# Attention heads of a two-layer encoder trunk: half a weight block of matmuls between the transposes of the two query halves

## The reference

```
for l in range(2):
    h = rms_norm(x, norm_mix_g[l])
    proj = h @ w_in[l]                      # lru_x, lru_g, dq, dk, dv, sq, sk, sv
    o_lru  = rglru_branch(...)
    # 8 differential heads, 64 wide in q and k, 128 wide in v
    p = softmax(mask(q @ k.T * scale + bias)); attn = p[0] - lam * p[1]; o_diff = attn @ v
    # 16 sliding-window heads in 2 groups, 64 wide, with a sink logit
    p = softmax(concat([q @ k.T * scale + bias, sink]))[..., :-1];      o_swa  = p @ v
    gates = sigmoid(h @ w_gate[l] + b_gate[l])
    x = x + sum(gates * (branches @ w_branch[l])) @ w_out[l]
    x = x + peer_ffn(rms_norm(x, norm_ffn_g[l]))
```

## Time and profile before

| | |
|---|---|
| median of 3 runs | 2584.67 us (2582.19 to 2586.20) |
| profiled execution, its own time | 2584.68 us |
| its span (first to last instruction) | 2582.5 us |
| PE busy, PEld busy | 94%, 87% of the span |
| DVE, ACT busy | 68%, 60% of the span |
| head stage of layer 0, T0 of head 0 to T0 of head 15 | 199.46 to 308.60 us |
| the same of layer 1 | 1485.19 to 1594.30 us |

### The profile page before, as it was taken

The page is one execution under the profiler, slowest core; times in us unless marked ns, Lnnn a source line. Parts: engine busy times, 40 slices in busy tenths (PEclk is TensorE's granted clock), DMA queues, the critical chain, the costliest instruction groups (busy, mean ns, idle before and its releaser), DMA issues.

```text
span 2582.5 us, 53628 instructions
## 1 busy us (share of the span) xinstructions
PE 2428.9 (94%) x16770; PEld 2237.4 (87%) x16770; DVE 1764.3 (68%) x4132; ACT 1558.0 (60%) x3530; POOL 31.1 (1%) x96
## 2 busy tenths in 40 slices
PE   8998999999999679999999999999999986899998
PEld 8997889999999568888899988899999985688887
DVE  5666764877765986666656667648777659766666
ACT  5567745655555865555555677455555558655555
POOL 0000100000000000000000001000000000000000
PEclk9999999999999999999999999999999999999999
DMA  6554444455554015555544443545555440255554
GB/s 216 190 180 131 133 161 169 163 183 185 184 172 153 0 68 193 194 195 195 194 153 168 168 147 121 174 147 180 186 187 179 167 142 0 96 190 190 191 194 170
DMA packets 116446, 413.66 MB, mean 160 GB/s; under 512 B 8028, under 2 KB 18196, under 8 KB 116116
## 3 DMA queue, kind: packets, MB, share of 16 engines
q1 hardware_dynamic: 115860, 412.44, 46.6%
q10 hardware_dynamic: 512, 0.29, 0.0%
HBM read 411.09 MB, written 4.23 MB: 161 GB/s over the span
## 4 chain that ended last, share of the span: by engine, by line
PE 83%; DVE 9%; ACT 4%; issue 3%; DVEq 1%; DMA 0%; ACTq 0%; POOL 0%; POOLq 0%
PE bank L282 16%; PE bank L284 16%; PE bank L283 16%; PE bank L297 10%; PE bank L298 9%; PE bank L299 9%; DVE hot L1427 3%; DVE w_lo L264 1%; DVE hot L1431 1%; ACT w_hi L251 1%; DVE A L1437 1%; PE bank L374 1%; ACT L324 1%; PE bank L1047 1%; DVEq L1431 1%
## 5 line engine op out<-in xcount | busy, mean ns | idle before, releaser
L264 DVE TENSOR_TENSOR w_lo<-raw,w_hi 128x512 fp32r<-128x512 f32 x1512 | 1028.1, 689 | 744.8 <-ACT w_hi L251 731.8
L251 ACT ACTIVATE w_hi<-raw 128x512 fp32r<-128x512 f32 x1512 | 905.3, 626 | 376.0 <-PE bank L299 310.6
L282 PE MATMUL bank<-h_hi,w_hi 128*128 128x256 f32 x3360 | 963.5, 287 | 14.1 <-DVE w_lo L264 14.0
L283 PE MATMUL bank<-h_lo,w_hi 128*128 128x256 f32 x3360 | 953.8, 284 | 0.0
L284 PE MATMUL bank<-h_hi,w_lo 128*128 128x256 f32 x3360 | 953.7, 284 | 0.0
L282 PEld LDWEIGHTS bank<-h_hi,w_hi 128*128 128x128 f32 x3360 | 647.2, 193 | 23.4 <-DVE w_lo L264 16.6
L283 PEld LDWEIGHTS bank<-h_lo,w_hi 128*128 128x128 f32 x3360 | 647.7, 193 | 0.5
L284 PEld LDWEIGHTS bank<-h_hi,w_lo 128*128 128x128 f32 x3360 | 647.5, 193 | 0.0
L297 PE MATMUL bank<-w_hi,a_hi 128*128 128x512 f32 x1088 | 425.4, 391 | 8.3 <-issue 5.0
L298 PE MATMUL bank<-w_lo,a_hi 128*128 128x512 f32 x1088 | 424.8, 390 | 0.0
L299 PE MATMUL bank<-w_hi,a_lo 128*128 128x512 f32 x1088 | 424.5, 390 | 0.0
(11 more groups left out here) (186 smaller groups left out, 1980.6 us busy)
## 6 DMA issues: line engine op xcount, KB each, us to landing
raw<-stream SPq DMA_DIRECT2D x378, 1024.0 KB, 4.9
hank<-rel_hankel SPq DMA_DIRECT2D x16, 256.0 KB, 2.7
rel_hankel<-rel_line SPq DMA_DIRECT2D x16, 192.0 KB
hank<-rel_hankel SPq DMA_DIRECT2D x16, 128.0 KB, 2.1
A<-subkeys SPq DMA_DIRECT2D x2, 1024.0 KB, 5.0
x<-x_in SPq DMA_DIRECT2D x2, 512.0 KB, 4.2
pr<-lru_w SPq DMA_DIRECT2D x2, 512.0 KB, 8.2
out<-x SPq DMA_DIRECT2D x4, 256.0 KB, 2.0
```

The source lines that it names most:

```text
L251: act.activation(w_hi[:, (ring % 2) * 2 + k, :], raw[:, slot, sub, 512 * k:512 * k + 512], ACT.Copy).then_inc(w_hi_done, 1)
L264: dve.tensor_tensor(w_lo[:, q, :], raw[:, slot, sub, 512 * k:512 * k + 512], w_hi[:, q, :].bitcast(F32), ALU.subtract).then_inc(w_parts, 1)
L282: pe.matmul(ps, hi, rhs_hi(4 * k + c), start=first, stop=False)
L283: pe.matmul(ps, hi, rhs_lo(4 * k + c), start=False, stop=False)
```

## The change

On PE, `transpose_p` takes the query half t as an argument. T0 is followed by half H, then comes T1, then half H+1. On ACT the read-out `read_turned` takes t as well: T0 is read, then `w_hi` of H' is made, then T1 is read. Nothing else moves, no instruction is added or removed, and DVE, POOL and SP are unchanged.

```diff
@@ ACT @@
-                def read_turned(m):
+                def read_turned(m, t):
...
-                    for t in range(TT):
-                        act.wait_ge(pt_done.sem, pt_done.base + 2 * m + t + 1)
...
+                    act.wait_ge(pt_done.sem, pt_done.base + 2 * m + t + 1)
...
-                    read_turned(m)
+                    read_turned(m, 0)
                     H = HALVES[m + 1]
                     split_to(H, H + 1)
+                    read_turned(m, 1)
                     if m < 15:
                         exps(m + 1, 0)
@@ PE @@
-                def transpose_p(m):
+                def transpose_p(m, t):
...
                     H = HALVES[m]
-                    transpose_p(m)
-                    halves(H, H + 2)
+                    transpose_p(m, 0)
+                    halves(H, H + 1)
+                    transpose_p(m, 1)
+                    halves(H + 1, H + 2)
                     values(m)
```

More of the change, by code:

```diff
@@ L672, in exps @@
                     ins.then_inc(exp_done.sem, 1)
-                def read_turned(m):
+                def read_turned(m, t):
                     swa = m >= HEADS_DIFF
-                    for t in range(TT):
-                        act.wait_ge(pt_done.sem, pt_done.base + 2 * m + t + 1)
-                        T = bank[6 + t][:, :].rearrange("p (a b) -> p a b", a=4)
-                        pick = (slice(0, 4) if t else slice(0, 4, 2)) if swa else slice(0, t + 1)
-                        act.activation(prob_t[:, t, pick, :], T[:, pick, :], ACT.Copy).then_inc(pt_read.sem, 1)
+                    act.wait_ge(pt_done.sem, pt_done.base + 2 * m + t + 1)
+                    T = bank[6 + t][:, :].rearrange("p (a b) -> p a b", a=4)
+                    pick = (slice(0, 4) if t else slice(0, 4, 2)) if swa else slice(0, t + 1)
+                    act.activation(prob_t[:, t, pick, :], T[:, pick, :], ACT.Copy).then_inc(pt_read.sem, 1)
                 def read_values(m):
@@ L1035, in scores @@
                             pe.matmul(bank[2 + 2 * s + c][:, P * t + lo:P * t + hi], q[r, P * t:P * t + P], k[r, lo:hi], start=True, stop=True).then_inc(scored.sem, 1)
-                def transpose_p(m):
+                def transpose_p(m, t):
                     s, swa = m % 2, m >= HEADS_DIFF
[L1040 to L1048, removed]
+                    pe.wait_ge(attn_done.sem, attn_done.base + 2 * m + t + 1)
+                    if m:
+                        pe.wait_ge(pv_read.sem, pv_read.base + 2 * (m - 1) + t + 1)
+                    for c in range(2 if swa else 1):
+                        for kt in range(t + 1):
+                            at = P * (2 * c + kt)
+                            ins = pe.transpose(bank[6 + t][:, at:at + P], prob(s, t)[:, c, P * kt:P * kt + P], ident)
+                    ins.then_inc(pt_done.sem, 1)
                 def values(m):
```

## The result

| | before | changed |
|---|---|---|
| median | 2584.1 us (2581.1 to 2586.4) | 2590.1 us (2587.5 to 2591.9) |
| ratio to before, 95% interval | | 1.0023 (1.0016 to 1.0030) |
| span of the profiled execution | 2582.5 us | 2586.6 us |

The kernel became slower by 6.0 us, 0.23%. Run again beside other kernels, the ratio was 1.0012 (1.0003 to 1.0021), so the size is known less well than the first interval says; the sign is not in doubt. The page hardly shows it: the busy shares are those of before.

A forecast was written before the change was run, and what follows sets the result against it. One loop through T1, ACT's list and `weigh_probs` sets each head's period, PE's branch being about equally long. Losses of 4.9 us in layer 0 and 4.4 in layer 1 make 9.3 us: 2594.0 us, range 2587.5 to 2600.

The forecast's parts named there:

- the second rival: Whole kernel: nothing measurable, since gate waits in heads 13 and 15 and low-clock stretches shrink; 2588.7 us; chance 0.10.
- One of the signs that the prediction named for being wrong: Differential heads, head stages: the prediction is wrong if their period stays at 7.25 us or falls.
- T0 to T1: Head stages: T0 to T1 becomes 1.60 us in differential heads (0.84 before), 1.70 in sliding-window heads (0.66 before).
- The upper end of 0.1 us a head: Half behind a single transpose: switch costs 0.20 us instead of 0.10, adding 2.8 us in both layers.
- PE's gain turns into a wait at T0: Differential heads: PE's shorter branch (3.30 us for 4.01) becomes idle time of about 0.6 us before T0.
- Differential heads: Heads 1 to 7: T1 0.76 us later less 0.52 of `w_hi`, 0.24 us a head, 1.7 us a layer.
- Sliding-window heads: Heads 8 to 12: period 7.41 us, losing 0.16 or 0.25 us each, together 1.1 us a layer.
- Head 13: T1 queued behind half H, which waits for DVE's gate product: 8.92 us against 7.87, 1.05 us lost.
- the third rival: More than forecast: one or two more lower-clock stretches at 1.49 us each and a dearer switch; 2599.8 us; chance 0.10.
- Heads 14 and 15: T0 of head 14 to values of head 15: gate product wait delays T1, 10.74 us against 9.89, 0.85 lost.
- Heads 0 and 1 of layer 1: Head 0 loses 0.7 us, about as much returns in head 1's lower-clock stretch; counted as 0.
- The decision point named there: Softer form of the first rival: T1 less than 0.52 us later, meaning a half in under 1.26 us, not 1.50.

The follow-up runs named there:

- PE's part alone: PE in the new order (T0, half H, T1, half H+1), ACT in its order of before, against the changed kernel; 2604.5 us, ratio to before 1.0075.
- kernel with these heads alone: The kernel before, with the new order of both engines in heads 13 and 15 only; 2587.4 us, ratio to before 1.0012.
- kernel with three groups: T1 after three of the four groups of half H, against the kernel with T1 in the middle of half H; 2575.3 us, ratio to before 0.9964.

## Why the prediction was right, and where its sum was off

The direction and the range held: 2590.1 us lies in 2587.5 to 2600, and slower by over 0.2% came true, though only just; in the second measurement it was 0.12%. That T1 heads ACT's list and ACT's list sets the next head is borne out by the runs that move T1. But the head stages grew by 5.0 us where the sum said 9.3, and without the stretch at the lower clock in head 13 of layer 1 by some 3.8. The measured time lies nearer to the second rival (2588.7 us) than to the forecast (2594.0), and that the clock took a further 1.2 us there, which the sum did not hold, was luck for the number.

One of the signs that the prediction named for being wrong came: the period of differential heads fell, from 7.25 to 7.20 us. In these heads the change costs nothing, and all of the loss lies in the sliding-window heads, most of it in heads 13 to 15.

- *T0 to T1.* Forecast 1.60 and 1.70 us, measured 1.61 and 1.71. A half behind a single transpose starts without any further price. The upper end of 0.1 us a head was not needed.
- *PE's gain turns into a wait at T0.* Forecast about 0.6 us idle there, measured 0.63. The kernel with PE's part alone shows it to the hundredth: 7.72 us.
- *Differential heads: the term that failed.* Forecast +0.24 us a head, measured -0.05. The working took over 0.71 us for the two read-outs of the values up to `w_hi` (226.62 to 227.33). In this 0.71 ACT waits about 0.2 for PE's second product, t=1. With PE ahead the pair takes 0.50. The source view of the two read-outs, before and in the changed kernel (ns of one: least, median, most; first and last start), shows them 0.45 us apart before and 0.25 after:

```profile
L691 ACT ACTIVATE o_own<-bank,small x2: 367/367/367, 226.6 to 227.1; 128x128 f32<-128x128 f32 x2
L690 ACT ACTIVATE o_own<-bank,small x2: 347/350/352, 227.4 to 227.7; 128x128 f32<-128x128 f32 x2
```

(The hundredths come from the earlier trace rows and the timeline after: the pair ends 0.81 us behind its start before, 0.60 after, and the last of it lasts 0.37 and 0.35.) For sliding-window heads the prediction saw the same wait, since there a row names it (0.20), and took it out; in differential heads the two read-outs stand in one merged row, x2 with 0.81 us, and it was missed. A second, smaller part: ACT starts the read-out 0.42 us behind T1 now, 0.48 before. Together that is 0.27 us, of the 0.29 by which a head was misjudged, in 13 heads 3.8 us.
- *Sliding-window heads.* Forecast 7.41 us, measured 7.33: 0.05 us from the same distance between T1 and its read-out (0.64 us for 0.69), 0.03 from the two read-outs of the values. Their loss was 0.6 us a layer, not 1.1.
- *Head 13.* Forecast 8.92 us, measured 8.78 in layer 0, and half H 1.68 us behind T0 for 1.71. The kernel with these heads alone gives 8.90 and 8.83. In layer 1 the changed kernel lost 1.2 us more to a stretch at the lower clock; such a stretch was part of the third rival, which put one or two at 1.5 us each.
- *Heads 14 and 15.* Forecast 0.85 us, measured 0.85 and 0.77.
- *Heads 0 and 1 of layer 1.* Forecast 0, measured -0.26: the stretch at the lower clock stayed in head 1, and PE's shorter branch hid half of it (8.03 us for 8.74).

Of the rivals, the first (PE's order sets the period, 2566 us) fell in its strong form. But its time was almost reached by the kernel with T1 in the middle of H, where both branches are shorter and ACT's list begins about when it did before: that is worth 0.4 to 0.7 us a head. It was the place of T1 that lost it. The busy share could not show this, since ACT's branch had to be shorter too. The decision point named there, a T1 less than 0.52 us later than before, was confirmed from the other side by the kernel with three groups: T1 0.40 us later than before, and a gain of 0.36%.

The second rival came nearest in time and was wrong in its reason. It took the gate heads to cost nothing and left 4.0 us for the rest; heads 13 to 15 cost 4.8 us in the profile, 1.2 of them from the clock, and the rest came out at 0.2 us.

## What to carry to other kernels

When work is put between two steps of a chain to fill an engine's idle time, its length has to be held against the idle time: 0.5 us of idle was filled here with 1.5 us of work, and everything that hangs on the second step moved back by the difference. With heads 13 and 15 left in the old order, that came out at nothing (0.9997), and filled with about 0.8 us the same gap gave 17 us. What the inserted work itself waits for moves ahead of the second step too, and as far as the times can tell this made up the loss. And where two branches of a loop are equally long, shortening one of them by itself is worth nothing (shown here for ACT's branch), while a merged row of two instructions can hide a wait between them: hold the distance between their starts against that of a pair that did not wait.

## What was not expected of the hardware

Head 13 of layer 1 ran partly at 1.2 GHz in both profiles of the changed kernel (granted clock 0.83 and 0.84 over the head) and took 10.0 and 10.3 us, while head 13 of layer 0, with the same instructions and (in the one shown) a wait of 1.24 us, took 8.8 us both times. With the same wait but the old order elsewhere it stayed at 2.4 GHz, and with PE's part alone it ran partly at 1.2 GHz in both layers (0.83). What tips it was not found.
